# Six of sixteen contraction tiles of the MLP pairs through seven products, in weight tiles of 1536 columns

## The reference

```python
for layer in range(2):
    h = h + mixer(rmsnorm(h, norm[layer]))                  # fox attention, then retention
    h = h + jnp.square(relu(rmsnorm(h, mlp_norm[layer]) @ w_up)) @ w_down   # 2048 -> 8192 -> 2048
return rmsnorm(h, final_norm)
```

## Time and profile before

| | us |
|---|---|
| median of 3 runs | 2487.61 |
| range of the runs | 2487.2 to 2490.51 |
| span of the profiled execution | 2485.3 |
| TensorE busy | 2474.5 |
| VectorE busy | 1915.0 |
| ScalarE busy | 1402.3 |
| GpSimd busy | 158.6 |

### The profile page before, as it was taken

How to read it: one execution, slowest core, us unless ns; L and a number is a source line. 1 busy time by engine, 2 the same in 40 slices (tenths; PEclk the granted TensorE clock), 3 DMA queues, 4 the chain that set the end, 5 groups by cost and what they waited for, 6 DMA issues and landing times.

```text
span 2485.3 us, 30031 instructions
## 1 busy us (share of the span) xinstructions
PE 2474.5 (100%) x11128; PEld 2050.7 (83%) x11128; DVE 1915.0 (77%) x2118; ACT 1402.3 (56%) x1689; POOL 158.6 (6%) x272
## 2 busy tenths in 40 slices
PE   9999999999999999999999999999999999999998
PEld 7888888888888888888888888888888888888887
DVE  6455555887978888987778868778988888788787
ACT  7454445554646555655556545656565555464564
POOL 0000000100100000101110001000010000010010
PEclk9999999999999999999999999999999999999999
DMA  8445456675756766766665665666677666666584
GB/s 312 158 155 182 140 200 218 214 253 182 260 202 222 248 208 229 237 212 204 219 225 184 231 201 183 199 206 233 236 248 245 207 231 229 211 237 237 192 273 146
DMA packets 148503, 534.83 MB, mean 215 GB/s; under 512 B 18704, under 2 KB 18960, under 8 KB 147472
## 3 DMA queue, kind: packets, MB, share of 16 engines
q1 hardware_dynamic: 131040, 476.65, 55.1%
q0 software_dynamic: 17184, 56.11, 7.9%
...
## 4 chain that ended last, share of the span: by engine, by line
PE 53%; DVE 2%; issue 1%; DMA 1%; ACT 1%; POOL 0%; DVEq 0%; ACTq 0%; POOLq 0%
PE acc L905 9%; PE acc L907 9%; PE acc L906 9%; PE sc L907 7%; PE sc L906 7%; PE sc L905 7%; PE mix L906 1%; PE mix L907 1%; PE mix L905 1%; DVE w_lo L1916 1%; ACT w_hi L1339 0%; DMA raw<-in_w_stream 0%; DMA evac<-park 0%; PE tr L1054 0%; PE tr L703 0%
## 5 line engine op out<-in xcount | busy, mean ns | idle before, releaser
L1916 DVE TENSOR_TENSOR w_lo<-raw,w_hi 128x1024 fp32r<-128x1024 f32 x696 | 847.1, 1230 | 290.4 <-ACT w_hi L1339 287.8
L1339 ACT ACTIVATE w_hi<-raw 128x1024 fp32r<-128x1024 f32 x696 | 727.8, 1058 | 571.8 <-PE sc L907 185.3
L905 PE MATMUL acc<-w_hi,xT_hi 128*128 128x512 f32 x826 | 322.6, 391 | 1.0 <-DVE xT_lo L1981 0.6
L907 PE MATMUL acc<-w_hi,xT_lo 128*128 128x512 f32 x826 | 321.6, 389 | 0.0
L906 PE MATMUL acc<-w_lo,xT_hi 128*128 128x512 f32 x826 | 321.5, 389 | 0.0
L1339 ACT ACTIVATE w_hi<-scratch 128x1024 fp32r<-128x1024 f32 x201 | 211.8, 1057 | 169.3 <-PE acc L907 74.4
L1916 DVE TENSOR_TENSOR w_lo<-scratch,w_hi 128x1024 fp32r<-128x1024 f32 x201 | 244.7, 1220 | 68.1 <-ACT w_hi L1339 67.5
L905 PE MATMUL sc<-w_hi,xT_hi 128*128 128x512 f32 x736 | 287.4, 390 | 0.0
L907 PE MATMUL sc<-w_hi,xT_lo 128*128 128x512 f32 x736 | 286.6, 389 | 0.0
L906 PE MATMUL sc<-w_lo,xT_hi 128*128 128x512 f32 x736 | 286.4, 389 | 0.0
L905 PE MATMUL acc<-w_hi,aT_hi 128*128 128x512 f32 x600 | 233.8, 390 | 0.0
(11 more groups left out here) (279 smaller groups left out, 3930.5 us busy)
## 6 DMA issues: line engine op xcount, KB each, us to landing
...
evac<-park POOLq DMA_DIRECT2D x152, 128.0 KB, 3.2
...
scratch<-qk_park POOLq DMA_DIRECT2D x32, 128.0 KB, 5.3
...
```

Source lines behind the costliest of these rows:

```text
L905: pe.matmul(bank[:, :], x_hi, w_hi[:, c], start=start, stop=False, skip_group_check=True)
L907: return pe.matmul(bank[:, :], x_lo, w_hi[:, c], start=False, stop=stop, skip_group_check=True)
L1339: act.activation(w_hi[:, slot * SW:(slot + 1) * SW], mlp_raw(u, load_of(u, t)), ACT.Copy).then_inc(mlp_hi, 1)
L1916: dve.tensor_tensor(w_lo[:, c], mlp_raw(u, load_of(u, t)), w_hi[:, c].bitcast(F32), ALU.subtract).then_inc(mlp_lo, 1)
```

## The change

It concerns 31 of the 32 MLP pairs (`WIDE_PAIR`, all but unit 0).

- Six contraction tiles of 16 go through the seven products: the left ones 0, 1, 4, the right ones 2, 3, 5. Each product has a weight tile of 3 contraction tiles, 1536 columns, 768 KB, and 9 matmuls. The ten other contraction tiles are in tiles of 3, 3, 2, 2 per block; in the first down pair behind two up pairs (`LATE`) and in unit 36 all are of 2.
- The weights of these pairs lie in a tensor of their own, `w_wide`, in the order of their use. There are five load slots of 1536 columns in the MLPs.
- The ring is counted in units of 512 columns: 14 in the MLPs, 12 in the retention layer. At units 16 and 36 counting starts anew at place 0.
- The products stand in the order B11, TAU1, TAU2, B21, TAU3, B22, TAU4. The shared sums are put into PSUM before a product is accumulated on them: ScalarE copies bank x to mix0 (`seed_u`), mix0 to bank z (`seed_z`) and mix1 to `junk` (`copy_p5`); VectorE writes bank e (`seed_e`, p5 less mix0) and bank w (`seed_w`, p5 less bank z). `u_part`, `v_part`, `g_part`, `fold` and `sum_to` are gone from the MLP pairs; the banks hold the results. `relu` and `relu_squared` replace `squared_relu` and `squared_relu_of_sum`.
- S1 to S4 take three tiles each, so they need two quads (`wide_sums` on quads 0 and 1 of a group). For the first down pair `s_high` and `s_low` stand at the end of the up pair ahead, in pieces of 256, 128 and 1152 columns.
- The gains are loaded in quads, into idle quads of `xT` and the ring's tail; POOL waits on `w_done` for each. Some scratch parts move there too.
- In the retention layer the pairs keep their widths and order; `wo_pair` is a function of its own.

In the pairs of the retention layer a pair has 186 matmuls as before; in a wide pair they are 7 x 9 + 20 x 6 = 183.

```diff
+LEFT, RIGHT = (0, 1, 4), (2, 3, 5)
+RING_UNITS_MLP, RING_UNITS_RET = 14, 12
+def place_tiles():
+    places, held, at = {}, {}, 0
+    for n, (u, t) in enumerate(ALL_TILES):
+        ring = RING_UNITS_RET if is_ret(u) else RING_UNITS_MLP
+        if t == 0 and u in (PAIRS, PAIRS + RET_UNITS):
+            at = 0
+        mine = [(at + k) % ring for k in range(width_of(u, t))]
+        at = (at + width_of(u, t)) % ring
+        before = [held[p] for p in mine if p in held]
+        places[u, t] = mine, ALL_TILES[max(before)] if before else None
...
 TensorE, wide_pair
+                block_sum(u, W_B11, x, lambda kk: x_part(lhs, 0, LEFT[kk]), True, True)
+                pe.wait_ge(s_lo, unit.sums)
+                wait(pe, p5_out, unit.wides)
+                block_sum(u, W_TAU1, mix[1], lambda kk: s_part(u, S1, kk), True, True)
+                pe.wait_ge(u_seeded, unit.wides + 1)
+                block_sum(u, W_TAU2, mix[0], lambda kk: s_part(u, S2, kk), False, True)
+                block_sum(u, W_B21, x, lambda kk: x_part(lhs, 0, RIGHT[kk]), False, False)
+                pe.wait_ge(z_seeded, unit.wides + 1)
+                block_sum(u, W_TAU3, z, lambda kk: s_part(u, S3, kk), False, True)
+                pe.wait_ge(e_seeded, unit.wides + 1)
+                block_sum(u, W_B22, e, lambda kk: s_part(u, S4, kk), False, False)
+                pe.wait_ge(w_seeded, unit.wides + 1)
+                block_sum(u, W_TAU4, z, lambda kk: x_part(lhs, 1, RIGHT[kk]), False, False)
...
 ScalarE, wide_pair
+                hi(u, W_TAU1)
+                hi(u, W_TAU2)
+                hi(u, W_B21)
+                if was_up:
+                    relu(0, e_done, sc[0], e_out, done, turn + 1)
+                    relu(1, w_done, sc[1], w_out, done, turn + 1)
+                    relu_squared(0, e_out, done)
+                seed_u(u, RET_HEADS * m)
+                hi(u, W_TAU3)
+                hi(u, W_B22)
...
+                copy_p5(u)
+                seed_z(u)
+                hi(u, W_TAU4)
...
 VectorE, wide_pair (turns, residual and norm in it left out)
+                lo(u, W_B11)
+                tau1(u)
...
+                    turn_blocks(turn)
+                tau3(u)
+                lo(u, W_TAU1)
+                tau2(u)
...
+                lo(u, W_TAU2)
...
+                lo(u, W_B21)
+                tau4(u)
...
+                lo(u, W_TAU3)
+                lo(u, W_B22)
+                seed_e(u)
...
+                lo(u, W_TAU4)
...
+                seed_w(u)
...
+                    turn_blocks(turn + 1)
+                lo(u, 7)
+                lo(u, 8)
...
+                        wide_sums(turn, 0)
+                    turn_lo(turn, *dst, p_quad)
...
+                        wide_sums(turn + 1, 1)
+                    turn_lo(turn + 1, *dst, p_quad + 1)
+                lo(u, last)
+                if new_sums:
+                    s_low(new_sums)
```

1010 lines of the change are left out of this document (607 added, 403 removed).

## The result

The changed kernel takes 2563.18 us (median of 4 runs, 2557.23 to 2569.38) against 2487.42 for the kernel before beside it (4 runs, 2487.2 to 2490.51): 1.0304 times the time, 95% interval 1.0286 to 1.0323. That is 75.8 us slower. I had forecast 11.4 slower and put the upper end of the range at 2512. The direction was right; the size was far off.

What follows compares the result with a forecast made beforehand. TensorE bounds the kernel: matmuls times their step. -21.1 + 13.6 + 7.8 + 9.3 + 1.8 = +11.4 us on the median 2487.6 gives 2499, range 2477 to 2512.

Steps and rivals of the forecast that it cites:

- The matmuls: All 31 changed pairs: 183 matmuls for 186, 93 fewer at 0.2267 us each, 21.1 us saved.
- The B pairs: Eight first down pairs behind two up pairs: TAU2 waits 1.7 us in each for the seed of u, 13.6 us.
- F: Landing of the second turned quad's fetch, counted from the up pair's start: 25.9 to 27.3 us, taken as 26.6.
- rival 4: TensorE's clock: three waits each send it to the lower level for 7 us, 10 us lost, 2510; chance 0.05.
- the third rival: Weight loads near DMA's limit: product tiles land 2 us late, 16 pairs around turns wait 2 us more, 2530; chance 0.05.
- Retention entry: Start of the retention layer: ring restart delays the first tile's copy and the chain behind it, 7.8 us lost.
- Last pair: Last pair of the first MLP: extra gains and a transpose on VectorE seed e and w late, 1.8 us.
- Exit: Pair after the retention layer: ring restart makes the products wait for late weight tiles and seeds, 9.3 us, between 7 and 11.
- Seeds: Shared sums put into PSUM ahead of products: in a pair without turned blocks all ready before need, cost 0.

Runs made afterwards that it cites:

- e3_light: Changed kernel; in the eight up pairs ahead of the first down pairs, each load behind the products moves only its first 128 columns: 2531.01 us (one run).
- e4_fill: Changed kernel with 14 matmuls, results thrown away, added ahead of TAU1 in each of the eight first down pairs: 2556.35 us (one run).
- e1: Changed kernel with the ring started at place 4 at unit 16 and place 8 at unit 36, not 0: 2554.34 us (one run).
- e6: Changed kernel with the ring started at place 4 at unit 16 and place 12 at unit 36, not 0: 2561.94 us (one run).
- e7: Changed kernel with the second turn made early and the ring started at places 4 and 12: 2537.6 us (4 runs), ratio 1.0198.
- e12_four: Changed kernel with four contraction tiles instead of six, weight tiles of 1024 columns and six load slots: 2518.14 us (4 runs), ratio 1.0124.

## Why the prediction was right and wrong

**The matmuls: right.** 93 fewer at a step of 0.2267. A pair without waits takes 41.57 us, 0.59 less than before (0.68 reckoned; the 0.09 are thirteen steps of 0.231 to 0.236 in TAU3 and B22, cause open).

**The B pairs: the step that failed.** The term was 13.6; over a quiet pair of 41.57 they took 53.6 more. By parts: TAU2's eight waits are 28.9 (2.0 to 4.3 each, reckoned 1.7); waits behind `aT_lo` and `h` later in the pair 6.0 (put at nothing); 61 steps at the lower clock 12.2 (put at nothing, named in rival 4); and 6.5 that stand beside these thirteen waits as restarts, the slower first steps behind a wait (put at nothing).

What failed first is F, the landing of the second quad's fetch: 27.5 to 30.5 us in the eight pairs, not 26.6. The start of the fetch was 0.1 to 1.1 late (18.9 to 19.9 for 18.8), since the park ahead of it took 5.4 to 7.0 us, which I had not priced. The landing of the last of the four issues took 6.7 to 9.1 us in place of 6.15. I had read the landing as 5.4 to 6.8 from the earlier trace rows. Those rows are medians of two issues; the last of the four landed after 5.5 us in the first and 7.6 in the third. And 26.6 is the middle of my 25.9 to 27.3, not "by the higher row"; that would have made 2.4 us per wait. Above all, the rows came from a kernel whose loads were spread over the pair; in the changed one the loads held back through the products come at once. e3_light takes them away, and F is 26.2 to 27.2 and TAU2's waits are 0.9 to 1.8.

I had named this as the third rival, "the product tiles land 2 us late", at a chance of 0.05, and set against it that product tiles have 4 us to spare. It was the wrong tile to look at: park and fetch have none. Rival 3's own sum of 378 GB/s wanted against 408 had already said that this queue is nearly full, and beside a fetch it moves less than 408. F alone is the smaller part: of the 40.0 us between 53.6 and 13.6, the longer waits at TAU2 are 15.3, clock and restarts 18.7.

**The clock: rival 4, true, at too low a chance.** It fell behind eight of the B pairs' waits, at both ends of the retention and in the last pair: 12 stretches, 93 steps of 0.43 us, 18.6 us. The prediction gave it 10 us for three waits, 3.5 each; that size had no row behind it, and measured are 1.2 to 2.2 per stretch. e4_fill shows that the idle time of PE brings it. The Trainium skill ("TensorE: Matmul & The Clock Gate", section "Why this matters for your kernels") warns of idle stretches between bursts of matmuls, and the trace after agrees: twelve of its fourteen waits over 2 us have slow steps behind them, and none of the shorter ones. The length alone does not decide it (last section).

**Retention entry: half right.** The wait for the ring's place was 2.50 (reckoned 2.6), and the chain behind the third quad's transpose ended 23.3 us into the block (22.0). Together with the wait of 2.88 at PE's transposes, which I had put into the chain only, and the clock, the stretch lost 17.8 for 8.9 reckoned with the last pair's term. **Last pair:** 1.8 reckoned, 2.37 and 1.23 measured, and its clock. **Exit:** 9.3 reckoned, waits of 6.6 measured (2.91, 1.18, 1.33, 1.14, where the first was to be 2.9), 10.4 with restarts and clock, net of the matmuls saved, of which 1.1 lie in the retention's last unit ahead. e1, e6 and e7 show the ring's place to be the cause of the first waits.

**Seeds: hidden, said the schedule; not quite.** e12_four has small waits of 0.2 to 0.6 in every pair behind seeds and low halves, where the schedule of the six-tile form had them 0.4 to 1.9 us ahead of need. With six tiles they mostly vanish in quiet pairs (0) and remain in the pairs behind B pairs (0.4 to 0.6).

**Open.** Why the loads take the engines' whole time at 270 to 372 GB/s is not shown. The stretches beside a fetch are the slowest in both kernels (318 at a share of 1.01 before), so the width of the tiles is not needed for it; no run takes the fetch away alone. What the waits behind `aT_lo` and `h` are due to was not tested. Not tried either: the six-tile form only in pairs without turns (by estimate 0.59 us each, some 9 us in 15 pairs), with the old form in the others. No version run was faster than the kernel before.
